# Conditioning products moved to the second feed-forward block and the first MLP, one or two at a time, with their sums in four column strips

## What is computed

```python
def conv_ffn(xn, w_up, conv_w, conv_b, w_down):          # feed-forward block, twice
    h = causal_dwconv(xn @ w_up, conv_w) + conv_b
    gate, val = h[..., :FFN_DIM], h[..., FFN_DIM:]        # FFN_DIM = 2816 = 22 chunks of 128
    return (jax.nn.silu(gate) * val) @ w_down

def second_block(x, c, ada_w, ada_b, ...):
    cond = jax.nn.silu(c)                                 # (1, 1024)
    for i in range(2):
        mod = cond @ ada_w[i] + ada_b[i]                  # ada_w[i]: 1024 x 6144
        sh1, sc1, g1, sh2, sc2, g2 = jnp.split(mod, 6)
        h = rmsnorm(x) * (1 + sc1) + sh1
        x = x + g1 * mixer_i(h)                           # i = 0: S5, i = 1: SSD
        h = rmsnorm(x) * (1 + sc2) + sh2
        x = x + g2 * (relu(h @ w1) ** 2) @ w2             # MLP, 1024 -> 4096 -> 1024
```

## Time and profile before

| | |
|---|---|
| median of three runs | 3426.83 us |
| span of the profiled execution (first to last instruction) | 3422.2 us |
| PE busy | 3113.5 us, 91% |
| DVE busy | 1811.9 us, 53% |
| POOL busy | 1397.7 us, 41% |
| ACT busy | 1049.2 us, 31% |
| mean granted clock of PE | 0.948 |
| POOL w_lo L231, 208 times | 969.4 us, 4661 ns each |
| DVE ada units L1129, 84 times | 166.1 us, 1977 ns each |
| DMA | 280.10 MB, mean 82 GB/s |

### The profile page before, as it was taken

How to read it: one execution, slowest core, us unless ns; L and a number is a source line. 1 busy time by engine, 2 the same in 40 slices (tenths; PEclk the granted TensorE clock), 3 DMA queues, 4 the chain that set the end, 5 groups by cost and what they waited for, 6 DMA issues and landing times. The chain is left out here.

```text
span 3422.2 us, 42075 instructions
## 1 busy us (share of the span) xinstructions
PE 3113.5 (91%) x15056; PEld 2424.1 (71%) x15056; DVE 1811.9 (53%) x2483; ACT 1049.2 (31%) x1419; POOL 1397.7 (41%) x581
## 2 busy tenths in 40 slices
PE   7999989999898999999865556999999999999998
PEld 6858967887777567887543334788887888578887
DVE  4435544547631654646799997632342239432324
ACT  4331222332333544332221211232223334322223
POOL 3324413444433013443346664433443349533442
PEclk9989999999999999999977887999999999999999
DMA  4310004446222114536220000323222220023322
GB/s 126 98 61 1 1 1 123 132 151 227 93 74 86 48 40 135 187 99 226 77 74 1 1 1 0 97 76 99 95 91 78 94 89 23 31 80 99 97 88 74
DMA packets 291923, 280.10 MB, mean 82 GB/s; under 512 B 10832, under 2 KB 275408, under 8 KB 291536
## 3 DMA queue, kind: packets, MB, share of 16 engines
q1 hardware_dynamic: 277968, 227.92, 21.6%
q10 hardware_dynamic: 13824, 50.34, 4.0%
HBM read 276.12 MB, written 2.10 MB: 81 GB/s over the span
## 5 line engine op out<-in xcount | busy, mean ns | idle before, releaser
L231 POOL TENSOR_TENSOR w_lo<-w_raw,w_hi 128x2048 fp32r<-128x2048 f32 x208 | 969.4, 4661 | 1549.0 <-ACT w_hi L203 1549.0
L240 PE MATMUL bank<-x_hi,w_hi 128*128 128x512 f32 x2048 | 810.2, 396 | 4.6 <-DVE h L399 4.6
L242 PE MATMUL bank<-x_hi,w_lo 128*128 128x512 f32 x2048 | 809.6, 395 | 0.0
L241 PE MATMUL bank<-x_lo,w_hi 128*128 128x512 f32 x2048 | 809.5, 395 | 0.0
L203 ACT ACTIVATE w_hi<-w_raw 128x2048 fp32r<-128x2048 f32 x208 | 398.1, 1915 | 982.6 <-PE bank L242 825.0
L240 PEld LDWEIGHTS bank<-x_hi,w_hi 128*128 128x128 f32 x2048 | 384.3, 188 | 100.7 <-DVE h L399 5.9
L241 PEld LDWEIGHTS bank<-x_lo,w_hi 128*128 128x128 f32 x2048 | 384.3, 188 | 93.9
L242 PEld LDWEIGHTS bank<-x_hi,w_lo 128*128 128x128 f32 x2048 | 384.2, 188 | 94.0
L1575 PE MATMUL bank<-pr,ck 128*32 128x128 f32 x1024 | 112.9, 355 | 144.1 <-DVE pr L1615 136.8
L1575 PEld LDWEIGHTS bank<-pr,ck 128*32 128x32 f32 x1024 | 91.7, 142 | 178.9 <-DVE pr L1615 150.3
L1144 DVE SCALAR_TENSOR_TENSOR y_gate<-bank,par,y_gate 128x511 f32<-128x511 f32 x88 | 65.9, 749 | 243.0 <-ACT y_gate L1087 236.8
(11 more groups left out here) (398 smaller groups left out, 5227.6 us busy)
## 6 DMA issues: line engine op xcount, KB each, us to landing
w_raw<-in_mlp_w SPq DMA_DIRECT2D x128, 512.0 KB, 4.3
ada_w<-in_ada_w ACTq DMA_DIRECT2D x96, 512.0 KB, 6.2
w_raw<-in_f_w_up SPq DMA_DIRECT2D x88, 512.0 KB, 5.0
w_raw<-in_m_w_in SPq DMA_DIRECT2D x40, 512.0 KB, 4.6
w_raw<-in_a_w_in SPq DMA_DIRECT2D x32, 512.0 KB, 5.0
w_raw<-in_f_w_down SPq DMA_DIRECT2D x32, 512.0 KB, 4.0
w_raw<-in_w_kv SPq DMA_DIRECT2D x16, 512.0 KB, 4.2
w_raw<-in_s_w_glu SPq DMA_DIRECT2D x16, 512.0 KB, 4.7
```

What stands on the lines that cost most here:

```text
L231: pool.tensor_tensor(w_lo[s][:, :], w_raw[s][:, :], w_hi[s][:, :].bitcast(F32), ALU.subtract).then_inc(lo_done, 1)
L240: pe.matmul(dst, hi_l, hi_r, start=start, stop=False)
L241: pe.matmul(dst, hi_l, lo_r, start=False, stop=False)
L242: return pe.matmul(dst, lo_l, hi_r, start=False, stop=stop)
```

## The change

The products of layer 0 move from feed-forward 0 to feed-forward 1, those of layer 1 from feed-forward 1 to MLP 0. Both are done one or two units at a time, ahead of the evacuation of a slot, in up slots too: in feed-forward 1 by the table `ADA_FFN`, in MLP 0 two in each of the 24 slots of the first three passes. The units go through a ring of 8 buffers of 512 KB, and ACT refills the place of a unit after its own work of that slot. The sums write to four strips of 32 partitions of one bank (`ADA_SUMS`), three matmuls each, the strip changing with every matmul; they stand after the second slot of the last down-projection, the turn (four 128 x 128 transposes into another bank) after the third, and `ada_mod_dve` between the third and the fourth add. Attention and the middle norm lose their sums and turns. The loops of feed-forward 1 (ACT, DVE) and of MLP 0 (ACT) are written out; `s_load_sp` waits for mod_done 3 in place of 6.

```diff
-        ADA_HALVES = (((0,), (1,), (2,), (3,)), ((4, 5), (6,), (7, 8), (9,)), ((10,), (11,), (), ()))
+        ADA_RING = 8
+        ADA_UNITS = 48
+        ada_w = [at(f"ada_w{r}", at_kb, [P, 1, D]) for r, at_kb in enumerate((80, 84, 88, 92, 96, 32, 36, 128))]
...
+        ADA_FFN = (((0, 1, 1, 2, 1, 2, 1, 2), (2, 2, 2, 2)), ((1, 2, 1, 2, 1, 2, 1, 2), (2, 2, 2, 2)), ((2, 2, 2, 2, 1, 1), (0, 0, 0, 0)))
+        ADA_MLP = 2
...
+        def ada_load_act(act, f, u):
+
+            ge(act, ada_used, ADA_UNITS * f + u - ADA_RING + 1 if u >= ADA_RING else 0)
+            w = t["ada_w"][f].rearrange("(k p) n -> p k n", p=P)
+            act.dma_start(ada_w[u % ADA_RING][:, :, :], w[:, u % KD:u % KD + 1, u // KD * D:u // KD * D + D]).then_inc(ada_in[u % KD // 4], 16)
+
+        def ada_unit_dve(dve, f, pc, k):
+
+            acc = ada_acc[:, ds(pc, 1), :]
+            if k % 4 == 0:
+                dve.wait_ge(ada_in[k // 4], 64 * pc + (64 * 6 * f + 64))
+            if k == 0:
+                dve.tensor_scalar(acc, ada_w[k][:, :, :], cond[:, 0:1], None, ALU.mult).then_inc(ada_used, 1)
+            else:
+                dve.wait_ge(ada_used, pc * KD + (ADA_UNITS * f + k))
+                dve.scalar_tensor_tensor(acc, ada_w[k][:, :, :], cond[:, k:k + 1], acc, ALU.mult, ALU.add).then_inc(ada_used, 1)
...
+                if f and c == 2:
+                    base = SLOTS[f"f{f}_dn{c}"]
+                    first_turn(pe, base, act_hi, act_lo, lambda k: (f_lo, 22 * f + F_START[c] + k + 1), F_CHUNKS[c],
+                               lambda k: (f_hi, 22 * f + F_START[c] + k + 1))
+                    ada_sums_pe(pe, 0)
+                    slot_body(pe, base + 2, act_hi, act_lo, F_CHUNKS[c], (0,))(0)
+                    ada_turn_pe(pe, 0)
+                    slot_body(pe, base + 3, act_hi, act_lo, F_CHUNKS[c], (1,))(0)
+                    continue
...
+        def ada_sums_pe(pe, f):
+
+            pe.wait_ge(ada_used, ADA_UNITS * (f + 1))
+            for i in range(3):
+                one = PAR["one_col"] + 31 - i
+                for q in range(4):
+                    r = 4 * i + q
+                    mm = pe.matmul(ADA_SUMS[32 * q:32 * q + 32, :], par[:, one:one + 32], ada_acc[:, r // 2, (r % 2) * T:(r % 2) * T + T],
+                                   start=(i == 0), stop=(i == 2))
+            mm.then_inc(ada_sum, 1)
...
+                    if c == 0:
+                        act.wait_ge(n_lo, KD * lots)
+                        for u in range(ADA_RING):
+                            ada_load_act(act, 0, u)
+                    for i in range(F_CHUNKS[c]):
+                        split_hi(act, base + i + 2, i % 2, landed(base + i - i % 2 + 2))
+                        up(i, i % 2)
+                        refill(0, i)
...
@@ attn_pe
-                if u < 6:
-                    ada_sums_pe(pe, 0, 2 * u, 2)
-                if u == 7:
-                    ada_turn_pe(pe, 0)
@@ mlp_act
+                if f == 0:
+                    for i in range(PASS):
+                        n = c * PASS + base + i
+                        split_hi(act, n + 2, i % 2, landed(n - i % 2 + 2))
+                        if i < 4:
+                            up(i, i % 2)
+                        for u in range(2 * (c * PASS + i), 2 * (c * PASS + i) + ADA_MLP):
+                            if u + ADA_RING < ADA_UNITS:
+                                ada_load_act(act, 1, u + ADA_RING)
+                        if c == 3 and i == 5:
+                            ada_rows_act(act, 1)
+                    return
@@ mlp_dve
+                        if f == 0 and not last:
+                            ada(c, i + s)
...
+                        if f == 0 and last and i + s == 2:
+                            ada_mod_dve(dve, 1)
@@ block.tensor
-            ada_sums_pe(pe, 1, 0, 12)
-            ada_turn_pe(pe, 1)
```

More of the change, by code:

```diff
@@ new lines, in build, with ada_start @@
+        ada_in = [sem(f"ada_in{r}") for r in range(2)]
+        ADA_FFN = (((0, 1, 1, 2, 1, 2, 1, 2), (2, 2, 2, 2)), ((1, 2, 1, 2, 1, 2, 1, 2), (2, 2, 2, 2)), ((2, 2, 2, 2, 1, 1), (0, 0, 0, 0)))
+        ADA_MLP = 2
+        def ada_start(c, part, i):
+            before = [ADA_FFN[d][p] for d in range(3) for p in range(2) if (d, p) < (c, part)]
+            return sum(sum(x) for x in before) + sum(ADA_FFN[c][part][:i])
+        def ada_load_act(act, f, u):
+            ge(act, ada_used, ADA_UNITS * f + u - ADA_RING + 1 if u >= ADA_RING else 0)
+            w = t["ada_w"][f].rearrange("(k p) n -> p k n", p=P)
+            act.dma_start(ada_w[u % ADA_RING][:, :, :], w[:, u % KD:u % KD + 1, u // KD * D:u // KD * D + D]).then_inc(ada_in[u % KD // 4], 16)
@@ L1042, in ffn_pe @@
                            ready_hi=lambda k: (f_hi, 22 * f + F_START[c] + k + 1))
-        ada_rows = at("ada_rows", 106, [32, T])
+        ada_rows = at("ada_rows", 76, [P, T])
         ada_sum, ada_row = sem("ada_sum"), sem("ada_row")
[L1048 to L1057, removed]
+        ADA_SUMS, ADA_TURN = bank[6], bank[7]
+        def ada_sums_pe(pe, f):
[7 more added lines that the diff above has]
+            mm.then_inc(ada_sum, 1)
         def ada_rows_act(act, f):
             act.wait_ge(ada_sum, f + 1)
-            act.activation(ada_rows[:, :], bank[5 + f][0:32, :], ACT.Copy).then_inc(ada_row, 1)
+            act.activation(ada_rows[:, :], ADA_SUMS[:, :], ACT.Copy).then_inc(ada_row, 1)
         def ada_turn_pe(pe, f):
@@ new lines, in ffn_act, with ada @@
+                for i in range(4):
+                    n = SLOTS[f"f{f}_dn{c}"] + i
+                    split_hi(act, n + 2, i % 2, landed(n - i % 2 + 2))
+                    if f:
+                        refill(1, i)
+                        if c == 2 and i == 1:
+                            ada_rows_act(act, 0)
+        def ffn_dve(dve, f, c_norm):
+            def ada(c, part, i):
+                if f:
+                    for u in range(ada_start(c, part, i), ada_start(c, part, i + 1)):
+                        ada_unit_dve(dve, 0, u // KD, u % KD)
+            if f:
+                dve.wait_ge(cond_in, 1)
@@ L1153, in up @@
                                           act_hi[:, ds(i + s, 1), :].bitcast(F32), ALU.subtract).then_inc(f_lo, 1)
-                turns(dve, F_CHUNKS[c], 2, up, peel=(f == 0 and c == 0))
+                if f == 0:
+                    turns(dve, F_CHUNKS[c], 2, up, peel=(c == 0))
+                else:
+                    for i in range(0, F_CHUNKS[c], 2):
+                        up(i)
                 base_dn = SLOTS[f"f{f}_dn{c}"]
@@ L1851, in mlp_dve, with ada @@
             base = SLOTS[f"p{f}"]
+            def ada(c, i):
+                for u in (ADA_MLP * i, ADA_MLP * i + 1):
+                    ada_unit_dve(dve, 1, 2 * c + u // KD, u % KD)
             def one(c, last=False):
@@ L1873, in down @@
                         n = c * PASS + (base + 4) + i + s
+                        if f == 0 and not last:
+                            ada(c, 4 + i + s)
                         for o in range(2):
```

110 lines of the change are left out of this document (44 added, 66 removed).

## The result

The changed kernel takes 3449.81 us (median of four runs, 3446.21 to 3453.01), the kernel before 3425.58 beside it (four runs, 3414.95 to 3428.2). The ratio is 1.0075, 95% interval 1.0062 to 1.0088: 0.75% slower, where the prediction had said 3399 us and faster. The profiled spans are 3422.2 before and 3448.9 after, +26.7.

What follows compares the result with a forecast made beforehand. PE, busy 91% of the 3422.2 us span, was taken as the bound. Terms -5.3 -8.2 -2.2 -5.0 -2.5 -10.6 -1.1 +7.4 = -27.5 gave a span of 3394.7, so 3399 us as run median, range 3384 to 3416.

Steps and rivals of the forecast that it cites:

- The failed step: Attention: removing sums saves 4.5 us, a low-clock restart costs about 2.35; net -2.2, bounds 0 and -4.5.
- sums and their turn gone: Attention: the fill no longer carries the sums spread over six units, -4.5 us before the clock's cost.
- Feed-forward 0: First feed-forward block, units gone: second down-projection -5.3 us, third -8.2 with its last square caught by w_lo.
- Rival (a): Last squares slip ahead of w_lo, MLP starts unstalled, attention gains its whole 4.5: total -39, 3388 us; chance 0.18.
- Feed-forward 1: Second feed-forward block: stalls go, -5.0 and -2.5 us; third down-projection with sums and turn -10.6, last square not caught.
- rival (b): Sum strips run one after the other, twice 8.6 us more: 3416 us, or 3413 at full clock; chance 0.13.
- the lower bound of 3.0: Sums in four strips: 3.0 us if fully side by side, 11.9 at most, 3.3 taken.
- Between the blocks: Middle norm: sums gone -2.6 us, low clock +2.0, DVE's earlier start of S5 -0.5; net -1.1, bounds 0 and -3.
- the 0.5 for the start of S5: Between the blocks: DVE loses three small ada_mod operations ahead of the S5 tables, so S5 starts sooner, -0.5 us.
- MLP 0: First MLP: start +3.5 us (bounds 0 and 6), sums in the last pass +3.3, turn +0.6; together +7.4.
- the prediction's rule: DVE throughout: an instruction with two SBUF inputs waits for a w_lo in flight, which runs 4.5 to 4.6 us.
- rival (c): Up slots of MLP and feed-forward: units caught by w_lo make DVE late, +28 us in all, 3455 us; chance 0.06.

Runs made afterwards that it cites:

- before_one_sum: Kernel before with 11 of the 12 sum matmuls of layer 0 in attention left out, one kept in the sixth unit: 3508.32 us.
- early_strips: Changed kernel with the first two bias strips loaded and masked earlier, so DVE can start with attention's first scores; no dummy matmuls: 3473.63 us.
- warm_wait: Changed kernel with 16 dummy fp32 matmuls of 512 columns in attention's units 0 and 1 and none behind them: 3490.04 us.
- warm_mid: Changed kernel with 12 dummy fp32 matmuls of 512 columns in units 26 and 27 of attention's 64, none at its start: 3434.47 us.
- early_eight: Changed kernel with early bias strips, MLP 0's first-slot units moved behind the squares, dummies in attention's units 0 and 1 only (unit 2's four left out): 3476.57 us.
- warm_mid_small: Changed kernel with 48 dummy matmuls of 128 columns in attention's units 26 and 27, in place of 12 of 512 columns: 3438.45 us.
- before_strips: Kernel before with only its sums changed to four column strips, at their old places: 3501.97 us.

## Why the prediction was wrong, step by step

**The failed step** is in the part on attention: "restarts after idle cost about 2.35 us of 192 matmuls ... Net -2.2; bounds 0 and -4.5". It saw that PE would idle and start at the low clock, and priced the return by the nearest restart, that of a projection. A projection is a dense stream of 128-row, 512-column matmuls; attention's is not, and the runs show that it does not lift a low clock as a projection does: it ran 221.9 us at 0.50 in before_one_sum and 204.8 in early_strips and warm_wait, and at 1.00 it ran 124.1 us in before and 82.8 in warm_mid once lifted. It is no strict hold: in after the clock rose by itself after 139.9 us, and in warm_wait and early_eight it fell among the loop's first tiles. The price is 7.38 against 13.40 us a head, 6.0 each: the 118 us between the start-up of the loop and the rise (1121.5 to 1239.4) are 8.8 heads at the low clock, 53 us by this estimate, where attention as a whole measured +51.9. The upper bound of 0 came from a restart elsewhere, which is no bound for a stretch with other work; the row that would have given one was in reach: 16 heads of 7.38 us, at half clock up to 118 us more. (The Trainium skill, "TensorE: Matmul & The Clock Gate", Part 1, has a busy engine back at full rate after a short sustained stretch; by it attention would have lost a few us. The traces disagree: PE was busy 204.8 of 204.8 us at 0.50 in warm_wait.)

A second omission made it possible: the prediction listed "sums and their turn gone" as pure gain and asked what they cost, and counted, of what they kept up, only this one restart. It did write that they "kept it busy", and of the middle norm that PE "kept the full clock because it did the sums", +2.0; the same thought stood one paragraph from the place where it was worth 52.

**Feed-forward 0: right.** -5.3, and -8.1 for -8.2 in its composition too: from first to last matmul 49.7 became 35.15 us, the 14.5 of the stall, and the norm behind gives 6.4 back, because the last square is caught as worked out (14.5 less 6.3 in the prediction). Timeline of after, beside the earlier trace rows:

```profile
937.38 4.50 POOL L231 TENSOR_TENSOR w_lo<-w_raw,w_hi 128x2048 fp32r<-128x2048 f32 x1 [3.75 <-ACT w_hi L203]
937.59 4.83 DVE L315 TENSOR_TENSOR sq_x<-h 128x512 f32<-128x512 f32 x1
942.48 1.87 PE L338 MATMUL bank<-ones,sq_x 128*128 128x1 f32 x8 [4.41 <-DVE sq_x L315]
```

Rival (a), that it slips ahead, did not happen; the square came 0.21 us behind the start of w_lo, where 0.05 had been worked out, so the side on which it fell was close.

**Feed-forward 1: right.** -7.5 and -10.9 for -7.5 and -10.6. The strips run side by side, and rival (b) is out:

```profile
1692.89 2.78 PE L1086 MATMUL bank<-ada_acc,par 128*32 128x512 f32 x24
...
1706.72 4.37 DVE L1205 SCALAR_TENSOR_TENSOR gain<-mod,par 128x8 f32<-128x8 f32 x1
...
1713.86 0.69 DVE L315 TENSOR_TENSOR sq_x<-h 128x512 f32<-128x512 f32 x1
```

24 records take 2.71 us from the first start to that of the next matmul, 0.113 each, under the lower bound of 3.0; the serial price at full clock, 0.43 a record, would be 10.3, so four strips are 3.8 times as fast. (The Trainium skill, "TensorE: Matmul & The Clock Gate", Part 3, gives 2.38 times for three column tiles, by which the prediction had an estimated 5.0 for four; no run here has three, and four measured 2.71 us.) A tiny operation of `ada_mod` was caught by w_lo (0.15 us of work, by its twin L1207, in 4.37), the last square was not, as forecast.

**Between the blocks: mis-sized.** -0.2 for -1.1. The sums of the norm behind (from their start to the spread's wait) took 4.14 us for 2.52 and the spread 3.82 for 2.90: the low clock cost 2.5, not 2.0. The waiting ahead of them shrank by 2.7, as forecast (2.6); the 0.5 for the start of S5 belongs behind this stretch, where 0.2 of it shows (from the projection to the first S5 matmul 51.1 before, 50.9 after).

**MLP 0: right in sum, in part by luck.** +7.0 for +7.4. The last down-projection cost +3.3 for 3.9, and the norm behind it, at the full clock nearly to its end (a spread of 1.16 for 2.07), got 0.9 shorter, which nobody had forecast; these two hide most of what the start cost too much. It cost +4.6 (predicted +3.5, bounds 0 and 6; PE's wait 2.8 for 2.2): the first unit waited for its load and then for w_lo, and PE for the relus behind it.

```profile
2259.96 4.61 POOL L231 TENSOR_TENSOR w_lo<-w_raw,w_hi 128x2048 fp32r<-128x2048 f32 x1 [20.00 <-ACT w_hi L203]
2260.79 4.33 DVE L1041 TENSOR_SCALAR ada_acc<-ada_w,cond 128x1024 f32 x1 [9.12 <-DMA ada_w<-in_ada_w]
```

This unit reads one SBUF tile (and a column of `cond`) and takes 0.75 alone, so the prediction's rule, that an instruction with two SBUF inputs waits for w_lo, was too narrow. And PE's waits there (total us, times, longest):

```profile
PE bank L240 <- DVE m_r L1913: 2.8, 1, 2.8
```

The other 28 slots ran without a stall, 44.80 for each four but for the sums. "Slower" had a chance of 0.06 in the prediction, all of it rival (c). The sign of that rival was right and its mechanism false: no unit of an up slot after the start held PE back. The true cause of slower was in no rival.

## What to carry over

Before moving or speeding up work on PE that seems free, ask which stretch starts right behind it and at what granted clock; a stream of small matmuls can stay at a low clock for 200 us. Price a possible clock change over the whole stretch, by one repeat at each level, and not by the restart of another stage. Where PE must wait ahead of such a stream, fill the wait and the first pauses with matmuls that nobody reads, spread over the stream's start and not only ahead of it: twelve here gave back 53 us.

## What the runs showed that was not expected

- The granted clock changes seldom in attention. In nine traces it was low for 88 us or more; in six of them it came back only in the last 15 us ahead of the projection behind attention, in the changed kernel after 139.9 us by itself, in warm_mid and warm_mid_small with the dummies. Why the changed kernel's rose at 1239.4 us in the middle of an unchanged stream stays open, and so does what in that stream (64-row scores, turned tiles, 64-column values) fails to lift the clock: none of them was tried alone.
- Small things decide over 50 to 90 us. Executions with one dummy more or less took 3395.61 and 3490.04 us, with four more or less 3391.37 and 3476.57, and executions of one and the same code 3393.61 and 3450.83. How much of this is chance in the clock at the start is open.
- Four column strips of fp32 matmuls in one bank, the strip changing with each matmul, ran 3.8 times as fast as one strip. In before_strips that speed was enough to bring the low clock.
